# Two projection chunks moved into the opening of a diffusion step, a new order of the scan steps, and a longer ring for the expert gather

## The reference, cut to what matters

```python
m = silu(cvec) @ ada_w + ada_b                      # 6 x 2048 modulation values per stream
h = rmsnorm(x, norm1_g) * (1 + sc1) + sh1
q, k, v, z, xbc, dt_raw, gates = split(h @ w_in)
na = attention(q, k, v)                             # 16 heads
ssd, s_f, s_b = ssd_branch(z, xbc, dt_raw)          # conv, SiLU, two scans, 8 groups, grouped norm
mixed = (g_na * (na @ w_na_proj) + g_ssd * (ssd @ w_ssd_proj)) @ w_out
x = x + g1 * mixed
h2 = rmsnorm(x, norm2_g) * (1 + sc2) + sh2
x = x + g2 * peer(h2)                               # per token 8 heads x 16 experts of 16384:
                                                    # act = gelu(u[e] . h2), sum of gate * act * v[e]
```

## Time and profile before

| | |
|---|---|
| median of 3 runs | 3198.01 us (3196.98 to 3202.96) |
| profiled execution | 3201.05 us |
| its span in the trace | 3198.6 us |
| TensorE matmul busy | 74% |
| VectorE busy | 72% |
| ScalarE busy | 36% |
| GpSimd busy | 38% |
| DMA, mean | 271 GB/s |

### The profile page before, as it was taken

The page is one execution under the profiler, slowest core; times in us unless marked ns, Lnnn a source line. Parts: engine busy times, 40 slices in busy tenths (PEclk is TensorE's granted clock), DMA queues, the critical chain, the costliest instruction groups (busy, mean ns, idle before and its releaser), DMA issues.

```text
span 3198.6 us, 38613 instructions
## 1 busy us (share of the span) xinstructions
PE 2356.6 (74%) x15046; PEld 2067.1 (65%) x15046; DVE 2287.7 (72%) x3020; ACT 1138.6 (36%) x1663; POOL 1203.4 (38%) x773
## 2 busy tenths in 40 slices
PE   6899999988888898999998910000122169998997
PEld 2688889987777797999987910000122158886886
DVE  1344447888888852444555899999999989885885
ACT  1233335544554452433333300000132194432333
POOL 0000000356555520000000022888888737664660
PEclk8899999999998999999999965555555579998999
DMA  9888875544444469776553477999999959996893
GB/s 404 314 305 295 291 281 200 176 150 144 140 144 144 152 212 353 267 268 227 189 196 132 145 252 248 410 422 422 422 421 421 381 166 363 367 347 238 324 367 135
DMA packets 149030, 866.73 MB, mean 271 GB/s; under 512 B 17857, under 2 KB 30161, under 8 KB 70625
## 3 DMA queue, kind: packets, MB, share of 16 engines
q1 hardware_dynamic: 67698, 447.32, 38.0%
q0 software_dynamic: 70992, 406.08, 33.0%
q10 hardware_dynamic: 10160, 10.88, 1.0%
HBM read 836.81 MB, written 27.39 MB: 270 GB/s over the span
## 4 chain that ended last, share of the span: by engine, by line
PE 54%; DVE 22%; issue 8%; DMA 7%; POOL 6%; ACT 3%; DVEq 0%; ACTq 0%; SPq 0%
PE bank L1657 30%; DVE u_ring L1533 10%; PE bank L1643 8%; PE bank L2019 7%; POOL u_ring L656 6%; DMA raw<-in_tiles 3%; PE bank L1682 2%; DMA v_got<-in_v_rest,expert 2%; DVE w_lo L1069 2%; PE bank L2002 2%; DVE peer_g L1562 2%; DVE hot_a L1550 1%; DMA u_ring<-in_peer_u,expert 1%; DVE conv L1183 1%; PE bank L1810 1%
## 5 line engine op out<-in xcount | busy, mean ns | idle before, releaser
L1069 DVE TENSOR_TENSOR w_lo<-raw,w_hi 128x1024 fp32r<-128x1024 f32 x482 | 640.7, 1341 | 573.2 <-ACT w_hi L698 565.9
L698 ACT ACTIVATE w_hi<-raw 128x1024 fp32r<-128x1024 f32 x482 | 502.4, 1057 | 716.3 <-PE bank L1657 378.0
L656 POOL DMA_INDIRECT u_ring<-in_peer_u,expert x256 | 505.9, 1976 | 403.7 <-PE bank L1657 212.8
L1657 PE MATMUL bank<-h_lo,w_hi 128*128 128x256 f32 x2048 | 594.1, 290 | 23.5 <-DVE w_lo L1069 15.2
L1533 DVE CUSTOM_DVE_ANT_0 u_ring<-u_ring,h_t 128x2048 f32<-128x2048 f32 x256 | 578.4, 2296 | 17.2 <-DMA u_ring<-in_peer_u,expert 15.9
L1657 PE MATMUL bank<-h_hi,w_lo 128*128 128x256 f32 x2048 | 582.2, 284 | 0.0
L1657 PE MATMUL bank<-h_hi,w_hi 128*128 128x256 f32 x2048 | 582.1, 284 | 0.0
L1657 PEld LDWEIGHTS bank<-h_lo,w_hi 128*128 128x128 f32 x2048 | 395.4, 193 | 65.6 <-issue 28.0
L663 POOL DMA_INDIRECT v_got<-in_v_rest,expert x256 | 340.1, 1329 | 231.9 <-DVE peer_g L1562 184.6
L1657 PEld LDWEIGHTS bank<-h_hi,w_lo 128*128 128x128 f32 x2048 | 395.7, 193 | 0.7
L1657 PEld LDWEIGHTS bank<-h_hi,w_hi 128*128 128x128 f32 x2048 | 395.2, 193 | 0.0
(11 more groups left out here) (301 smaller groups left out, 4567.9 us busy)
## 6 DMA issues: line engine op xcount, KB each, us to landing
raw<-in_tiles SPq DMA_DIRECT2D x337, 1024.0 KB, 5.3
v_raw<-in_v_dense SPq DMA_DIRECT2D x128, 660.0 KB, 7.1
s_t<-in_states POOLq DMA_DIRECT2D x8, 512.0 KB, 6.9
y_hi_rows<-y_hi_e POOLq DMA_DIRECT2D x16, 256.0 KB, 2.4
y_lo_rows<-y_lo_e POOLq DMA_DIRECT2D x16, 256.0 KB, 3.4
gate_rows<-gate_buf ACTq DMA_DIRECT2D x8, 512.0 KB, 4.8
y_hi<-y_hi_rows POOLq DMA_DIRECT2D x1, 4096.0 KB, 27.2
y_lo<-y_lo_rows POOLq DMA_DIRECT2D x1, 4096.0 KB, 16.7
```

The costliest lines, as they stand in the source:

```text
L656: pool.indirect_dma_start(u_ring[s][:, e % U_RING], None, a["peer_u"][0], bass.IndirectOffsetOnAxis(ap=expert[:, s, k:k + 1], axis=0)).the ...
L698: act.activation(w_hi[:, i % RING], raw[:, slot % SLOTS, (n % 2) * 2 * CH:(n % 2 + 1) * 2 * CH], ACT.Copy) \
L1069: dve.tensor_tensor(w_lo[:, i % RING], raw[:, n // 2 % SLOTS, (n % 2) * 2 * CH:(n % 2 + 1) * 2 * CH], w_hi[:, i % RING].bitcast(F32), ALU. ...
L1657: ins = pe.matmul(spot if x.shape[1] == KT else spot.rearrange("p (s t) -> p s t", s=NS), w[:, col], moving, start=start and k == 0 and m ...
```

## The change

The order of the spine: q0 and k0 are placed tile by tile among the modulation chunks i = 3, 5, 7 and 9; chunk i = 8 comes alone, v0 is paired with i = 10, and the rest as before. Each q0 and k0 tile waits for its own block of h only. Modulation sums use banks 4 and 5 (and are turned into the same bank), x is turned in banks 6 and 7. The steps of the scan move by up to three halves on the three engines. The first stream's gathers use 14 slots (`U_FIRST`), the second's eight others. `hot_a` of stream 0 is made on ScalarE.

```diff
     for q in range(4):
         alone("ada", q)
-        alone("ada", 4 + q)
-    for j in range(4):
+        if q:
+            seq.extend((("ada", 4 + q, 0), ("q", 0, q - 1), ("ada", 4 + q, 1), ("ada", 4 + q, 2), ("k", 0, q - 1),
+                        ("ada", 4 + q, 3)))
+        else:
+            alone("ada", 4)
+    alone("ada", 8)
+    seq.extend((("q", 0, 3), ("ada", 9, 0), ("ada", 9, 1), ("k", 0, 3), ("ada", 9, 2), ("ada", 9, 3)))
+    paired("v", 0, 10)
+    for j in range(1, 4):
...
+        n = e % U_FIRST if e < SEL else U_RING + e % U_RING
+        slot.append(n)
+        turn.append(len(users.get(n, [])))
+        last.append(users[n][-1] if n in users else None)
...
-        u_ring = [at(f"u_ring{s}", [P, U_RING, D], F32, 64 * s) for s in range(NS)]
+        u_ring = at("u_ring", [P, 2 * U_RING, D], F32, 0)
...
-        ada_bank = lambda i: psum[i % 2] if i < 8 else psum[4]
-        turn_spot = lambda i: psum[2 + i % 2][:, 0:8] if i < 8 else psum[4][:, 0:8]
+        ada_bank = lambda i: psum[4 + i % 2] if i < 8 else psum[4]
+        turn_spot = lambda i: ada_bank(i)[:, 0:8]
...
-                if e >= U_RING:
-                    pool.wait_ge(u_used, e - U_RING + 1)
+                if U_LAST[e] is not None:
+                    pool.wait_ge(u_used, U_LAST[e] + 1)
...
```

ScalarE's `scan`, and its new part of `one_hot`:

```diff
-                    if t == 0 and g:
-                        result_hi(g - 1, 1)
-                    elif t == 1:
+                    if t == 1:
                         decays(g, 0)
                     elif t == 2:
                         turned_xs(g, 0)
+                        if g:
+                            result_hi(g - 1, 1)
                     elif t == 4:
                         turned_xs(g, 1)
-                    elif t == 6:
+                    elif t == 7:
                         decays(g, 1)
-                    elif t == 8:
+                    elif t == 10:
                         norm(g, 0)
-                    elif t == 10:
+                    elif t == 11:
                         final_states(g)
-                    elif t == 11:
+                    elif t == 13:
                         result_hi(g, 0)
-                    elif t == 14:
+                    elif t == 15:
                         norm(g, 1)
...
+                if s == 0:
+                    for n in range(BATCH):
+                        ins = act.activation(hot_a[:, q % 2, n], iota_r[:], ACT.Abs, scale=-1.0,
+                                             bias=pick_t[:, 0, b * BATCH + n:b * BATCH + n + 1])
...
```

VectorE's `scan`, TensorE's `scan`, and the waits:

```diff
-                    if t == 0 and g:
+                    if t == 3 and g:
                         result_lo(g - 1, 1)
-                    elif t == 3:
-                        products_copied(g)
                     elif t == 4:
                         from_states(g)
                     elif t == 5:
+                        products_copied(g)
+                    elif t == 6:
                         mix(g, 0, 0)
                         mix(g, 0, 1)
-                    elif t == 6:
+                    elif t == 7:
                         decayed(g)
                         skipped(g, 0)
-                    elif t == 7:
+                    elif t == 9:
                         combine(g, 0)
-                    elif t == 8:
+                    elif t == 10:
                         skipped(g, 1)
-                    elif t == 10:
+                    elif t == 11:
                         mix(g, 1, 0)
-                    elif t == 11:
                         mix(g, 1, 1)
-                    elif t == 12:
+                    elif t == 13:
                         result_lo(g, 0)
-                    elif t == 13:
+                    elif t == 14:
                         combine(g, 1)
...
                 elif t == 1:
+                    if g:
+                        turn_result(g - 1, 1)
                     xs_turned(g, 0)
-                elif t == 2:
-                    products_bc(g)
                 elif t == 3:
                     with_states(g)
                     xs_turned(g, 1)
-                elif t == 5:
+                elif t == 4:
+                    products_bc(g)
+                elif t == 6:
                     segments(g, 1)
-                elif t == 6:
+                elif t == 8:
                     products(g, 0)
                 elif t == 9:
                     final_states(g)
-                elif t == 10:
+                elif t == 12:
                     turn_result(g, 0)
-                elif t == 12:
+                elif t == 13:
                     products(g, 1)
-                elif t == 15:
-                    turn_result(g, 1)
...
-                    elif c == 0:
-                        pe.wait_ge(nt_lo, 4)
+                if kind in ("q", "k") and j == 0 and h % 2 == 0:
+                    pe.wait_ge(nt_lo, h // 2 + 1)
...
-                    if i == 1 and h in (1, 3):
-                        norm_turn(0, h // 2, x_t)
-                    if i in (3, 5) and h == 1:
-                        norm_turn(0, (i + 1) // 2, x_t)
-                    if i == 7 and h == 7:
-                        ada_turned(7)
+                    if i in (1, 3, 5, 7) and h == 1:
+                        norm_turn(0, i // 2, x_t)
...
```

More of the change, by code:

```diff
@@ L109, with ring_slots @@
 WINDOWS = GROUPS + 1
+def ring_slots():
+    slot, turn, last, users = [], [], [], {}
+    for e in range(NS * SEL):
+        n = e % U_FIRST if e < SEL else U_RING + e % U_RING
+        slot.append(n)
+        turn.append(len(users.get(n, [])))
+        last.append(users[n][-1] if n in users else None)
+        users.setdefault(n, []).append(e)
+    return slot, turn, last
+U_SLOT, U_TURN, U_LAST = ring_slots()
 def accumulators():
@@ L416, in program @@
         x2_saved = sem("x2_saved")
-        u_in = [sem(f"u_in{n}") for n in range(U_RING)]
+        u_in = [sem(f"u_in{n}") for n in range(2 * U_RING)]
         u_used = sem("u_used")
@@ L865, in side @@
                             .then_inc(rms_done, 1)
-                    if i < 8 and i % 2 == 0 and i >= 2 and h == 4:
+                    if i <= 8 and i % 2 == 0 and i >= 2 and h == 4:
                         modulated_hi(0, i // 2 - 1)
@@ L921, in side @@
                     ins.then_inc(evac_a, 1)
-                elif kind == "gates" and j == 2 and h == 0:
+                elif kind == "gates" and j == 2 and h == 2:
                     result_hi(GROUPS - 1, 1)
@@ L1023, in one_hot @@
                                          bias=pick_t[:, 1, b * BATCH + n:b * BATCH + n + 1])
+                if s == 0:
+                    for n in range(BATCH):
+                        ins = act.activation(hot_a[:, q % 2, n], iota_r[:], ACT.Abs, scale=-1.0,
+                                             bias=pick_t[:, 0, b * BATCH + n:b * BATCH + n + 1])
                 link(ins)
-                act.activation(hot_b[:, q % 2], hot_b[:, q % 2], ACT.Relu, scale=-1.0, bias=1.0).then_inc(key_ready, 1)
+                ins = act.activation(hot_b[:, q % 2], hot_b[:, q % 2], ACT.Relu, scale=-1.0, bias=1.0)
+                ins.then_inc(key_ready, 1)
+                if s == 0:
+                    link(act.activation(hot_a[:, q % 2], hot_a[:, q % 2], ACT.Relu, scale=-1.0, bias=1.0))
+                    for n in range(BATCH):
+                        ins = act.activation(hot_a[:, q % 2, n], hot_a[:, q % 2, n], ACT.Copy,
+                                             scale=pick_t[:, 2, b * BATCH + n:b * BATCH + n + 1])
+                    ins.then_inc(hot_scaled, 1)
             for s in range(NS):
@@ L1105, in modulate @@
                         b = 4 * q + k
-                        bank = psum[4 + 2 * (q % 2) + k // 2]
+                        bank = psum[4 + 2 * (q % 2 if norm else 1) + k // 2]
                         at_ = (k % 2) * T + s * P
@@ L1386, in side @@
                         diagonals(0, 2)
-                    if 0 < i < 8 and h == 2:
+                    if 0 < i <= 8 and h == 2:
                         mod_sum(i - 1)
-                    if i < 8 and i % 2 == 0 and i >= 2:
+                    if i <= 8 and i % 2 == 0 and i >= 2:
                         q = i // 2 - 1
@@ L1439, in side @@
                     convolve("bc", 3, h)
-                elif kind == "gates" and j == 2 and h == 0:
+                elif kind == "gates" and j == 2 and h == 3:
                     result_lo(GROUPS - 1, 1)
@@ L1500, in side @@
                     mod_sum(8 + 3 * j + "qkv".index(kind) - 1)
-                if kind == "k" and j == 0 and 1 <= h < 5:
+                if kind == "v" and j == 0 and 1 <= h < 5:
                     bias_sum(h - 1)
@@ L1590, in _ @@
                 expert_act(SEL + k)
-                if k >= 16 and (k - 16) % 3 == 0 and (k - 16) // 3 < BATCHES:
-                    one_hots(0, (k - 16) // 3)
             coefficients(1)
@@ L1699, in norm_turn @@
             def norm_turn(norm, q, x):
-                if q >= 2:
+                if norm == 0 and q:
```

(6 more changed lines are left out.)

51 lines of the change are left out of this document (24 added, 27 removed).

## The result

| | before | after |
|---|---|---|
| median of the runs, us | 3199.23 (3196.98 to 3202.96) | 3156.8 (3154.59 to 3158.49) |
| profiled execution, us | 3201.05 | 3154.59 |
| its span, us | 3198.6 | 3152.7 |

A forecast was written before the change was run, and what follows sets the result against it. It took DMA to bound the opening and most of the gather, TensorE between, except in scan windows. Gains of 6.2, 21 and 18.4 us from 3201.05 gave 3155.5, or 3152 us from the median; range 3134 to 3174.

The forecast's parts named there:

- The opening: Start up to v0: projection tiles among DMA-bound modulation tiles start v0 at 158.5 us, 6.2 us gained.
- the scan: Scan windows: reordered steps shorten the TensorE and VectorE loop by 3.0 us in each of 7 windows, 21 us.
- the gather: Expert gather: fourteen slots gain 14.9 us before the first Gelu; with one-hots off VectorE, 18.4 us in all.
- the cycle: Opening: ten tiles (ada, q, k) take 31.1 us a cycle, putting tile 42 at 135.7 us.
- the tail: Opening, last tiles before v0: 17.4 us, plus 2.4 for a low-clock first tile and 3 for cache loads.
- Rival 2: Opening: it overlaps wholly, v0 at 133 to 138 us, 23 us more gained, 3129 us; chance 0.07.
- my lower end, 67.7 us: Scan: window length if the wait breaks in two and the low clock ends before the products; otherwise 69.3 us.
- moving `combine` would win nothing: Scan: if VectorE and GpSimd only locked each other out for whole instructions, the gain would be 2.7 us per window less.
- Rival 1: Scan: the stall only moves, so the 21 us are not gained, 3173 us; chance 0.12.
- Rival 4: Scan window's end: norm, SiLU, `z_g` and split stand exposed, 10.2 us lost per window, 3244 us; chance 0.06.
- rival 3: Gather: extra gathers not issued early or GpSimd descriptors limit; only the one-hots' 3.5 us stays, 3167 us; chance 0.07.
- Nothing elsewhere: Stretches outside opening, scan windows and expert gather were priced at no change.

The follow-up runs named there:

- e9: The changed kernel with its three 1 MB cache loads issued one each at rows 1, 2 and 3, not all at row 4: 3147.93 us, ratio 0.9856.
- e7: The changed kernel leaving out two of the three products in the first six q and k tiles (result wrong): 3146.23 us, ratio 0.9854.
- e1: The kernel before with the new order of the scan steps alone: 3164.65 us, ratio 0.9896.
- e12: The kernel before with only a group's second row turn moved, from half 15 to half 1 of the next window: 3246.92 us, ratio 1.0157.
- e2: The kernel before with the 14-slot ring and the first stream's one-hots on ScalarE alone: 3180.59 us, ratio 0.9940.
- e5: The kernel before with the 14-slot ring for the first gather stream alone, one-hots still on VectorE: 3184.53 us, ratio 0.9950.
- e14: The changed kernel with a group's second row turn put back in half 15: 3207.79 us, ratio 1.0031.

## Why the prediction was right, and where it was wrong

**Sum.** 45.6 us were forecast between the two profiled executions and 45.9 measured. The opening was 13.6 us worse than forecast, the scan 10.2 better, the gather 2.5 worse; the dense stage's scatter gave the other 6. That they cancel is luck.

**Opening: the cycle nearly right, the tail and the sign wrong.** Tiles 12, 22, 32 and 42 land at 42.4, 74.2, 106.8 and 139.1 us: 32.2 a cycle for 31.1, so 3.4 us of the error are in three cycles. The forecast had 22.8 us from tile 42 to v0 and the trace has 30.2, another 7.4. (1) The caches: 3 us were put down, "an estimate between 0 and 7.5". From tile 42 to v0 it is 24.0 us in e9, so they cost 6.3 there, and with 1 us more ahead of tile 42 in e9 v0 gains 5.3. (2) The other 4 us are mostly splits: 3.5 us and not 2.4 ahead of q, 1.2 more ahead of k, and 1.2 ahead of v0 where 1 us was taken off. (3) v0's own tile at the lower clock, 2.75 us, counted nowhere. That makes the 13.6. I had noted a loss of up to 8 us as the bound; it is what came. The 5.2 us of the earlier trace rows are no load with an empty queue either: two more were issued 0.7 and 1.3 us behind it, and the shortest of the 337 tile loads took 4.6 us, near the other estimate in the prediction, 4.4. With the caches out of the way (e9), the interleaving is worth 1.9 us against the mean of the old openings, about their scatter. Rival 2, a complete overlap, is refuted by the cycle, and by e7: even a third of the products left 28.2 us.

**Scan: the mechanism right, the size too small.** 5.0 us a window came, where 3.0 was forecast and 4.5 was the most allowed. The wait was broken in two as described, 2.9 us at the row turn ("some 4") and up to 3.0 at the products ("1 to 3"), and the low clock was over before the products. That was my lower end, 67.7 us; I took the middle, and this is the step that was mis-sized. The rest is VectorE's chain from half 4 to the end of the second mix, 38.9 us in the forecast. Half 4 ends where `products_bc` (L1818) starts, at 913.81, and the mix ends at 951.30: 37.5. Its first piece was right, the first mix ends 8.2 behind half 4 for 8.4; the largest single difference is a split of 2.3 us for 2.9.

For VectorE beside GpSimd the prediction read the rows as a stretching, against the whole lock-out of two-input instructions that the Trainium skill states (SBUF - State Buffer, SBUF: two separate sides). The trace agrees with the skill. The split of 930.59 begins while GpSimd works until 932.31, and ends at 933.40, 1.09 us later; alone, at 947.69, it takes 1.22. All 48 splits between 620 and 1190 us that begin beside one of GpSimd's mask operations end 1.08 to 1.09 us behind the end of that operation; in the kernel before there are 58, and all end 1.08 us behind it. A convolution step, which reads a PSUM bank, takes 0.47 us beside GpSimd or without. So what was wrong is the prediction's step from the lock-out to "moving `combine` would win nothing": behind the first mix VectorE's chain took 29.3 us where it had taken 32.7, with steps of the convolution beside GpSimd where `combine` and `skipped` had been.

Of 5.0 us x 7 windows 3.9 came back behind the last window; why is not tested. Rival 1 (the stall only moves) is refuted by e1. Rival 4 (the chain at the window's end exposed) did not come about: the new wait for the convolved rows is 0.9 us a window. But its price, 3244, is nearly what e12 measured, by another wait (3247).

**Gather: right, 15.9 us for 18.4.** Choosing to first Gelu is 14.3 us shorter (14.8 in e2 and e5), for 14.9; e5 shows that this is the ring's, and rival 3 fell. The second stream runs at 320.0 / 128 = 2.50 us a gather for 2.485, so 1.6 us of 3.5 came: the term was mis-sized, as the second stream had run at 321.6 / 128 = 2.51 us a gather with the one-hots on VectorE.

**Nothing elsewhere** held for the stretch from `out` to the choosing, to 0.1 us. My line of 3 us for the dense stage was no test: it scatters by more.

## What to carry to other kernels

Price a move by the bank and the ring slot it occupies until it's used, as well as by its engine time: here two parts of a new order, of which each alone costs 2 to 7 us a window, gain 5 together. When transfers are moved into an engine-bound stretch, look at what else is issued at its end: three unhurried loads in one burst cost 8 us, and the interleaving gained 2 at most. And compare stretches between landmarks before you call a forecast right: the total came out within 5 us with one of three terms of the wrong sign.

## What the runs showed of the hardware

VectorE's instructions with two SBUF inputs and GpSimd's mask operations take turns, one whole instruction at a time: a 128x1024 split that begins beside one ends 1.08 us behind its end, up to 2.9 us after its own start, for 1.22 alone. An instruction that reads PSUM goes through at its usual time (0.47 us).

Three 1 MB loads issued together with tiles land 5.4, 7.1 and 10.9 us later, and a tile issued behind them takes 14.05 us, where the shortest tile load took 4.6. That queueing by itself is no loss; the engine lost at most 7.5 of it. The granted clock made stalls dearer than their length: with a wait of 4.3 to 7.5 us more in each window (e14) TensorE's busy time for the same matmuls was 63.4 us against 60.4 in the windows shown, and behind the 5.5 us wait ahead of v0 its first tile took 2.75 us longer.
